# Attention's product with the values: turned so that the split exponentials are stationary and the split values move, with the seam before attention reordered

## The reference

```
def token_mixing(h, ...):
    z = h @ w_in
    qa, ka, va, cq, ckv, kr = split(z)
    qa, ka = rope(rmsnorm(qa)), rope(rmsnorm(ka))         # 8 query heads, 2 key heads, 64 wide
    oa = window_attention(qa, ka, va, swa_sink)           # keys of the tile before, the same and the next
    qb = (rmsnorm(cq) @ mla_w_uq)                         # 8 heads, 96 wide
    kv = (rmsnorm(ckv) @ mla_w_ukv)                       # k_nope and vb, 64 wide each
    kb = concat(k_nope, k_rope)
    qb, kb = rmsnorm and rope of both
    ob = dense_attention(qb, kb, vb)
    return concat(oa, ob) @ w_out

y = (silu(h @ wg) * (h @ wu)) @ wd                        # SwiGLU, before and behind; x += gate * y each time
```

## Time and profile before

| | |
|---|---|
| time, three runs | 3287.0 us median (3283.91 to 3290.35) |
| the profiled execution | 3284.61 us, span of the trace 3282.8 us |
| granted TensorE clock over the span | 0.983 of full speed |
| busy: PE / PEld / DVE / ACT / POOL | 96% / 75% / 44% / 25% / 16% |
| DMA | 207.51 MB, 63 GB/s mean |
| mixing by tiles | about 1280 to 1492 us |
| attention | about 1512 to 2033 us |
| output projection | from 2036 us |

### The profile page before, as it was taken

How to read it: one execution, slowest core, us unless ns; L and a number is a source line. 1 busy time by engine, 2 the same in 40 slices (tenths; PEclk the granted TensorE clock), 3 DMA queues, 4 the chain that set the end, 5 groups by cost and what they waited for, 6 DMA issues and landing times.

```text
span 3282.8 us, 39034 instructions
## 1 busy us (share of the span) xinstructions
PE 3156.4 (96%) x14017; PEld 2456.1 (75%) x14017; DVE 1458.5 (44%) x2512; ACT 809.3 (25%) x1422; POOL 522.0 (16%) x307
## 2 busy tenths in 40 slices
PE   7999999999999989996989998999999999999998
PEld 2688888888888868884545555878888888888887
DVE  2566666666662356874443332362322232322234
ACT  3311111011111145763433333331111111111112
POOL 1111111111111143320000001531111111111110
PEclk9999999999999999997989999999999999999999
DMA  7112122221221022445312122221011111011112
GB/s 245 39 57 69 40 77 66 62 64 55 60 67 37 27 79 63 139 138 138 91 39 60 50 69 74 84 71 33 26 38 32 32 32 32 26 38 32 32 32 84
DMA packets 268288, 207.51 MB, mean 63 GB/s; under 512 B 16956, under 2 KB 241071, under 8 KB 268207
## 3 DMA queue, kind: packets, MB, share of 16 engines
q1 hardware_dynamic: 268206, 206.41, 21.4%
HBM read 169.31 MB, written 37.06 MB: 63 GB/s over the span
## 4 chain that ended last, share of the span: by engine, by line
PE 53%; DVE 4%; issue 2%; ACT 1%; SPq 1%; DMA 1%; DVEq 0%; POOL 0%; ACTq 0%
PE PS L428 13%; PE PS L429 13%; PE PS L430 13%; PE PS L1454 6%; PE PS L1405 1%; PE PS L1439 1%; PE PS L1438 1%; PE PS L1440 1%; PE PS L1418 1%; DVE mbuf L1573 1%; PE PS L1394 1%; PE PS L1430 0%; SPq L1688 0%; PE PS L1431 0%; PE PS L1461 0%
## 5 line engine op out<-in xcount | busy, mean ns | idle before, releaser
L428 PE MATMUL PS<-H_hi,W_hi 128*128 128x512 f32 x2304 | 906.5, 393 | 8.0 <-POOL W_lo L1771 4.1
L430 PE MATMUL PS<-H_hi,W_lo 128*128 128x512 f32 x2304 | 898.5, 390 | 0.0
L429 PE MATMUL PS<-H_lo,W_hi 128*128 128x512 f32 x2304 | 897.9, 390 | 0.0
L422 POOL TENSOR_TENSOR W_lo<-raw,W_hi 128x1024 fp32r<-128x1024 f32 x132 | 316.1, 2402 | 1829.4 <-ACT W_hi L395 1829.4
L578 DVE SCALAR_TENSOR_TENSOR XT<-PS,mod,XT 128x512 f32<-128x512 f32 x528 | 395.4, 750 | 302.9 <-PE PS L430 302.7
L428 PEld LDWEIGHTS PS<-H_hi,W_hi 128*128 128x128 f32 x2304 | 433.7, 188 | 99.3 <-issue 11.1
L430 PEld LDWEIGHTS PS<-H_hi,W_lo 128*128 128x128 f32 x2304 | 433.3, 188 | 92.0
L429 PEld LDWEIGHTS PS<-H_lo,W_hi 128*128 128x128 f32 x2304 | 433.8, 188 | 90.0 <-issue 1.4
L564 DVE TENSOR_TENSOR PS<-hid_g,PS 128x512 f32<-128x512 f32 x132 | 91.8, 696 | 821.5 <-PE PS L430 810.4
L395 ACT ACTIVATE W_hi<-raw 128x1024 fp32r<-128x1024 f32 x132 | 137.2, 1055 | 1225.2 <-PE PS L430 1224.4
L428 PE MATMUL PS<-hid_hi,W_hi 128*128 128x512 f32 x1056 | 416.3, 394 | 6.5 <-DVE XT L578 5.1
(11 more groups left out here) (207 smaller groups left out, 3028.5 us busy)
## 6 DMA issues: line engine op xcount, KB each, us to landing
ada_r<-in_ada_w SPq DMA_DIRECT2D x192, 128.0 KB, 2.3
raw<-in_ffn_wg SPq DMA_DIRECT2D x44, 512.0 KB, 3.9
raw<-in_ffn_wu SPq DMA_DIRECT2D x44, 512.0 KB, 4.0
raw<-in_ffn_wd SPq DMA_DIRECT2D x44, 512.0 KB, 3.6
ada_w_sb<-in_ada_w SPq DMA_DIRECT2D x6, 2048.0 KB, 15.5
raw<-in_w_out SPq DMA_DIRECT2D x24, 512.0 KB, 4.2
scr_qb<-qT_st SPq DMA_DIRECT2D x24, 384.0 KB, 4.7
scr_kb<-kT_st SPq DMA_DIRECT2D x24, 384.0 KB, 6.2
```

What stands on the lines that cost most here:

```text
L422: pool.tensor_tensor(W_lo[:, n % WS, :], raw[:, n % RS, :], W_hi[:, n % WS, :].bitcast(F32), ALU.subtract).then_inc(w_ready, 1)
L428: pe.matmul(out, w_hi, m_hi, start=first, stop=False)
L429: pe.matmul(out, w_hi, m_lo, start=False, stop=False)
L430: return pe.matmul(out, w_lo, m_hi, start=False, stop=last)
```

## The change

The product with the values is turned round. The exponentials `e` are split into `p_hi` (ACT, a second pass) and `p_lo` (POOL, a subtraction), and the values into a high and a low part; for each 128 queries `p_hi` or `p_lo` is the stationary side and 66 or 64 columns of values move. The output lies with queries on partitions, so that the copy and the four transposes of the accumulator are gone. The product lags three steps where it lagged two. The low part of the dense values is made by DVE in the mixing stage and stored beside the high part (`VHL` = 130 columns a head instead of 66); the window values are split by POOL after their load. Room for the new buffers is found in `XT`: it is saved tile by tile to DRAM during mixing, and loaded back (two tiles at unit 8, the rest in the output projection). In SP's plan the window loads move behind `sp_m`, and the query loads behind `sp_t`; the transposes of the last tile's q and k move behind the first row maxima. ACT's copy of the values waits for the saving of the first two tiles, and `dve_turn` of unit 0 for the values' writes. The first unit's two pieces of maxima use different banks.

```diff
-QR, PR, MR = 4, 3, 5
+QR, MR = 4, 5
+ER, HR = 3, 4
+PV_LAG = 3
+VHL = 2 * VB + 2
...
 def act_m(act, u):
...
+            act.wait_ge(xt_kept, 32)
+            act.activation(vb_hl[:, :, 0:VB], kv[:, :, NOPE:NOPE + VB], ACT.Copy).then_inc(*aM.tick("v_copied"))
...
 def dve_m_norm(dve, u):
...
+            dve.wait_ge(aM.sem, aM.at(u, "v_copied"))
+            dve.tensor_tensor(vb_hl[:, :, VB + 2:VHL], kv[:, :, NOPE:NOPE + VB], vb_hl[:, :, 0:VB].bitcast(F32),
+                              ALU.subtract).then_inc(*vM.tick("v_lo"))
             dve.wait_ge(aM.sem, aM.at(u, "k_square"))
...
+        def sp_keep(sp, u):
...
+            sp.dma_start(scr_xt[bass.ds(u, 1)].rearrange("a p k c -> p (a k) c"), XT[:, :, tok(u)]).then_inc(xt_kept, 16)
...
-            turns(sp, [(sp_rope, 0), (sp_ropeb, 1), (sp_swa, 1), (sp_m, 2), (sp_t, 2), (sp_s, 1), (sp_z, 0)])
+            turns(sp, [(sp_rope, 0), (sp_ropeb, 1), (sp_m, 2), (sp_swa, 1), (sp_t, 2), (sp_swa_q, 1), (sp_s, 1), (sp_z, 0), (sp_keep, 0)])
...
 def pe_values(pe, un, t):
-            pe.wait_ge(exps_done, i + 1)
-            if t == 0 and un.u >= 1:
-                pe.wait_ge(acc_kept, un.u)
+            pe.wait_ge(p_lo_done, i + 1)
...
-            pe.matmul(PS[0:VW, 4, :], v, probs[:, i % PR, :], start=(t == 0), stop=(t == un.nk - 1)).then_inc(pv_done, 1)
-
-        def pe_back(pe, un):
...
+            if first and un.u >= 2:
+                pe.wait_ge(o_scaled, un.u - 1)
             for q in range(4):
-                mm = pe.transpose(PS[:, 5, q * VW:(q + 1) * VW], acc[0:VW, un.rd, q * P:(q + 1) * P], ident[0:VW, 0:VW])
+                out, by = PS[:, 4 + un.rd, q * VW:(q + 1) * VW], slice(q * P, (q + 1) * P)
+                pe.matmul(out, p_hi(i)[:, by], v_hi, start=first and q == 0, stop=False, skip_group_check=True)
+                pe.matmul(out[:, 0:VB], p_hi(i)[:, by], v_lo, start=False, stop=False, skip_group_check=True)
+                mm = pe.matmul(out, p_lo(i)[:, by], v_hi, start=False, stop=last and q == 3, skip_group_check=True)
+            mm.then_inc(pv_done, 1)
...
 def attention_pe(pe):
...
+            for i in range(N_ALL):
+                if i < len(steps):
+                    un, t = steps[i]
+                    pe_scores(pe, un, t)
+                if i < len(steps) and t == 0 and un.u + 1 < NU:
                     pe_max_turn(pe, units[un.u + 1])
+                if PV_LAG <= i < len(steps) + PV_LAG:
+                    pe_values(pe, *steps[i - PV_LAG])
+                for v in units:
+                    if i == done_at(v.u) + 2:
+                        pe_turn(pe, v)
+                for ahead, piece in maxes_at(i):
+                    pe_max(pe, ahead, piece)
...
 def act_exp(act, un, t):
+            if i >= ER:
+                act.wait_ge(p_lo_done, i - ER + 1)
+            act.activation(e_slot(i), PS[:, 2 + i % 2, :], ACT.Exp).then_inc(exps_done, 1)
+
+        def act_p_hi(act, i):
+            act.wait_ge(exps_done, i + 1)
+            if i >= HR:
+                act.wait_ge(pv_done, i - HR + 1)
+            act.activation(p_hi(i), e_slot(i), ACT.Copy).then_inc(p_hi_done, 1)
...
-        def act_acc(act, un):
...
 def attention_pool(pool):
...
+            swa_v_split(pool, 0, NT - 1)
+            for i, (un, t) in enumerate(steps):
...
+                pool.wait_ge(p_hi_done, i + 1)
+                if i >= HR:
+                    pool.wait_ge(pv_done, i - HR + 1)
+                pool.tensor_tensor(p_lo(i), e_slot(i), p_hi(i).bitcast(F32), ALU.subtract).then_inc(p_lo_done, 1)
...
 def swa_loads(sp):
...
+            sp.wait_ge(xt_kept, 16 * NT)
             swa_tiles(sp, 0, NT - 1, swa_landed)
-            for un in units[0:QR]:
-                load_q(sp, un)
...
 def attention_loads(sp):
...
+                    for t in range(2):
+                        sp.dma_start(XT[:, :, tok(t)], scr_xt[t]).then_inc(xt_front, 16)
...
 def wo_loads(sp):
...
+                if 1 <= i <= KD:
+                    if i == 1:
+                        sp.wait_ge(pv_done, len(steps))
+                    sp.dma_start(XT[:, i - 1, CH:TOK].rearrange("p (t c) -> p t c", c=P),
+                                 scr_xt[TPC:NT, :, i - 1, :].rearrange("t p c -> p t c")).then_inc(xt_back, 16)
```

More of the change, by code:

```diff
@@ L83, in build @@
         silu_c = sb(ctx, "silu_c", [P, KD, 2])
+        with ExitStack() as sX:
+            XT_r = sb(sX, "XT_r", [P, KD, TOK], F32R)
         XT = sb(ctx, "XT", [P, KD, TOK])
@@ L1271, in sp_swa, with sp_swa_q @@
                 swa_loads(sp)
+        def sp_swa_q(sp, u):
+            if isinstance(u, int) and u == NT - 1:
+                for un in units[0:QR]:
+                    load_q(sp, un)
         def turns(eng, plan, done=()):
@@ L1286, in turns @@
                 for stage, lag in plan:
-                    if 0 <= u - lag < NT:
+                    if 0 <= u - lag < NT and (stage, u - lag) not in done:
                         stage(eng, u - lag)
@@ L1360, in build, with done_at @@
         turn_no = {un.u: i for i, un in enumerate(turns_out)}
+        def done_at(u):
+            return last_step[u] + PV_LAG
+        N_ALL = len(steps) + 8
         def turns_until(u):
@@ L1380, in v_job, with max_bank, maxes_at @@
             return un.seq * (HB // 2) + un.head // 2
+        def max_bank(un, piece):
+            return 2 * piece if un.u == 0 else 0
+        def maxes_at(i):
+            if i >= len(steps) or steps[i][0].u + 2 >= NU:
+                return []
+            (un, t), ahead = steps[i], units[steps[i][0].u + 2]
+            return [(ahead, piece) for piece in range(ahead.pieces)
+                    if t == (piece + 4 if un.nk == 8 else min(piece, un.nk - 1))]
         def pe_max(pe, un, piece):
             a = maxes_before[un.u] + piece
-            if a >= 1:
-                pe.wait_ge(reds_done, a)
+            if a >= 2:
+                pe.wait_ge(reds_done, a - int(a == 2))
             pe.wait_ge(un.q_sem[un.slot], q_count(un.u))
             if un.swa and NT - 1 in un.keys:
-                pe.wait_ge(swa_last, 16 * 8)
+                pe.wait_ge(swa_last, 16 * 6)
             if un.swa:
@@ L1481, in attention_pe @@
             pe.wait_ge(ones_rows, 2)
[L1482 removed]
+            pe.wait_ge(swa_landed, 16 * 6)
             for un in units[0:2]:
@@ L1550, in attention_act @@
             act.wait_ge(sw_written, 16 * (NT + 1))
-            for un, t in steps:
-                act_exp(act, un, t)
-                if t == 0 and un.u + 1 < NU:
-                    act_max_row(act, units[un.u + 1])
-                if t == 1 and un.u >= 1:
-                    act_acc(act, units[un.u - 1])
-                if t == 1 and un.u >= 3:
-                    act_turn(act, units[un.u - 3])
-                if t == un.nk - 1 and un.u + 2 < NU:
-                    act_sink(act, units[un.u + 2])
-            act_acc(act, units[-1])
-            for un in units[-3:]:
-                act_turn(act, un)
+            for i in range(N_ALL):
+                if i < len(steps):
+                    un, t = steps[i]
+                    act_exp(act, un, t)
+                    if t == 0 and un.u + 1 < NU:
+                        act_max_row(act, units[un.u + 1])
+                    act_p_hi(act, i)
+                    if t == un.nk - 1 and un.u + 2 < NU:
+                        act_sink(act, units[un.u + 2])
+                for v in units:
+                    if i == done_at(v.u) + 3:
+                        act_turn(act, v)
         def dve_max(dve, un, piece):
```

160 lines of the change are left out of this document (83 added, 77 removed).

## The result

Measured in alternation, the changed kernel takes 3741.2 us (median of 4 runs, 3735.8 to 3748.0) and the kernel before 3287.3 (3283.9 to 3290.4): a ratio of 1.138, 95% interval 1.137 to 1.139. The forecast was 3367, with a range that ended at 3465. The profiled execution took 3744.7 us (span 3742.9).

The account below looks back on a forecast made before the run. The prediction took TensorE to bound the kernel, setting the time of attention's 224 steps. Its terms, 103 - 12 - 12 - 9 + 6 + 3 + 3 = +82 us on 3284.6, gave 3367 us, range 3320 to 3465.

Parts of the forecast that it names:

- The product: Attention, value product: 12 matmuls at 0.110 us, 1.32 us per step in place of 0.86; +103 us over 224 steps.
- the cheaper load: Rival, value product: new stationaries load in 0.062 us like the accumulator's transposes; about 3239 us, chance 0.10.
- the shared load: Rival, value product: the pair on one stationary shares a load, 1.0 us per step; 3295 us, within break-even's chance.
- no overlap: Rival, value product: load and stream do not overlap, 0.14 us per matmul; 3448 us, chance 0.04.
- break-even: Rival, value product: loads partly hidden, spacing near 0.08 us per matmul; 3286 us, no change, chance 0.05.
- The clock: TensorE in attention: forecast clock 1.00; rival has a third of steps at the lower level, about 3520 us, chance 0.07.
- Accumulator and unit changes: Attention: four transposes per unit go, -12 us; TensorE's waits for row maxima and o_sb shrink, -7 us.
- The 5 us that the clock was to give back: Around 1677 to 1703 us: half-speed stretches behind TensorE's waits shorten as the waits shrink; -5 us.
- ACT and POOL: Attention: second ACT pass and one POOL subtraction (1.30 us) per step lie beside TensorE's 2.02 us step; 0 us.
- The seam: Before attention: writes come first, query load is late next, from 1497; -9 us (-15 to +5), first exponential near 1515.
- The smaller additions: DVE subtraction in mixing +6 us, XT copies 0, loads at unit 8 +3, output projection and end of attention +3.
- The sum: Whole kernel: all terms together +82 us on the profiled 3284.6 us, giving 3367 us; forecast's chance 0.74.

Follow-up runs that it names:

- the run with twice the columns: Changed kernel with each value matmul streaming its moving tile a second time into unused columns of its bank; 3458.3 us, ratio to the kernel before 1.052.
- paired run: Changed kernel with TensorE's order alone altered: score passes of two steps together, then the value products of two steps; 3661.5 us.
- the XT-copies run: Kernel before plus only the writes of each XT tile to DRAM during mixing, read by nothing; 3287.4 us against 3289.0, ratio 0.9996.
- the mixed one: Changed kernel with TensorE's order alone altered: a step's value matmuls stand between its three score passes (3, then 6, then 3); 3743.1 us.
- the one with the long wait shortened: Changed kernel with the two loads of XT's front tiles issued after the last key and value load; 3730.0 us.
- the version as a whole: Changed kernel with values stationary again, split exponentials streaming 512 columns, XT front loads later, prompt-unit maxima one step earlier; 3256.5 us, ratio to the kernel before 0.990.
- the runs with more columns: Changed kernel with value tiles streamed twice (3458.3 us), first score pass issued three times (3551.9), or value tiles streamed twice and first score pass issued twice (3493.6).
- both additions: Changed kernel with each value matmul streaming its columns twice and the first score pass of a step issued twice; 3493.6 us.

## Why the prediction was wrong

**The product: right.** 12 matmuls at 0.11 us and a step near 2.0 (measured 2.06). A unit of 8 steps grew from 16.0 to 19.7 us on average (the latter in the run with twice the columns), 3.7 us; the forecast had 8 x 0.46 less 0.25 for the transposes, 3.4. That run shows that the 0.11 is the load's. This speaks against the cheaper load, the shared load, no overlap and break-even alike. The Trainium skill's 81 ns for a pair at 128 columns ("TensorE: Matmul & The Clock Gate", "Back-to-back issue gap") does not hold for this form: 0.11 us at 2.4 GHz, in the run with twice the columns at just those 128 columns, and 0.21 at 1.2.

**The clock: this step failed.** The forecast took 1.00 through attention. It had the mechanism among its rivals ("most of a step is loads with short streams, and no row has that"), but gave it 0.07, with a third of the steps and 3520 us as its far end. Measured are, after 1540 alone, 850 of the 963 us from first score to last product at 0.50, 380 us of loss. Even the far end of that rival fell 221 us short. Two readings led there. It argued from the waits, which would shrink, and took -5 us for it. The waits did shrink (next point), and TensorE was busy for 98% of the stretch at 0.50. And the step's time at the low level was put at twice 2.02 for a third of the steps, without a reason for a third. The steps of a stage are alike, so nothing in the rows bounded the case below the whole stage: all 224 steps at the low level would have given 224 x 2.02 = 452 us more, by the forecast's own price. The share of the load records is no sign either: in mixing they cover 105 of 120 us at 1.00, with 256 columns behind each load, and in the new stretch at 0.50 they cover 452 of 522, with 66. The prediction wrote down that no row had steps of this kind, and then gave that little weight. The Trainium skill ("TensorE: Matmul & The Clock Gate", "Part 1: The HAM clock gate") says that the clock follows how busy the engine has been. The paired run's 88 us, all busy and at 0.50, do not agree if busy is what the profile's row calls busy.

**Accumulator and unit changes: right in size, as far as it can be read.** The kernel before waited in attention 11.4 + 8.6 us in the earlier trace rows, and 6.5 more for maxima and sinks before L1418. The changed one waits 12.4 for maxima and sinks and 0.7 for o_sb, with 5.4 for H_lo where it was 1.5: some 10 less, against the 7 taken. At the low clock TensorE leaves the other engines more time, so part of this may be the clock's: in the run with twice the columns, mostly at 1.00, these waits come to 22.5, which is 5.5 less. The 5 us that the clock was to give back have the wrong sign.

**ACT and POOL: right.** The low part takes 1.27 us a step on POOL, and no product waited for it.

**The seam: too hopeful by 5.** The rows around it (as the earlier trace rows):

```profile
1502.41 0.60 ACT L1078 ACTIVATE XT_r<-PS 128x512 fp32r<-128x512 f32 x1 [0.17 <-PE PS L456]
...
1502.52 5.60 SPq L1296 DMA_DIRECT2D scr_qb<-qT_st  x2
...
1509.85 1.49 POOL L1722 CAST swa_v<-XT 128x704 fp32r<-128x704 f32 x2 [13.26 <-DMA XT<-scr_va]
1510.24 9.39 SPq L1761 DMA_DIRECT2D q_swa<-scr_sw  x12
...
1516.78 0.55 PE L1455 MATMUL PS<-swa_ka,q_swa 128*128 128x256 f32 x1 [14.40 <-DMA q_swa<-scr_sw]
...
1529.68 0.60 ACT L1580 ACTIVATE XT<-PS 128x512 f32<-128x512 f32 x1 [1.39 <-PE PS L1492]
```

ACT's wait of 11.56 is gone (0.17), as predicted, and the query load is late next, as predicted; but it is issued at 1510 and not at 1497: the window loads end at 1502 and the four writes of tile 10 take 7.7 us, not 5. TensorE waits 14.4 us for it. From the last transpose of the latents to the first exponential it is 48.4 us where it was 52.1: 4 gained, not 9. The first exponential is at 1529.7, not near 1515, because the mixing also ends later.

**The smaller additions.** Mixing: +4.0 of the +6 taken, none of it the copies; the rest of the part is DVE's subtraction and the wider value write, not separated. The mixing also began 5 us later in this execution, which no step explains; in the XT-copies run it began 2.7 us later with no loss of time in the end. The burst of loads at unit 8: 5.7 us against 3 (0 to 8). At the output projection the first matmul waits 4.1 us for W_lo in both kernels.

**The sum** without the clock: 3364 measured so, 3367 forecast; the run with twice the columns gives 3361, the paired one 3346, the mixed one 3354 and the one with the long wait shortened 3352, each profiled time less 0.45 of its time at 0.50. So one price explains all of them. That the sum of the parts comes within 3 us is in part luck. The first exponential came 5.3 us later (1529.7 against 1524.4), where the seam and mixing terms had it 3 earlier. From the first to the last exponential the kernel before takes 501 us; the changed one, with the loss at 0.50 taken off, some 566, so +65 (+73 in the run with twice the columns), where the terms for attention add up to +82. These misses go opposite ways.

## What to carry to other kernels

Before turning a product so that the long side becomes stationary, count columns streamed per load in the new step, and treat the TensorE clock as a term of the sum that can take the whole stage, not as a side case: it cost here 380 us, where all the rest of the change cost some 80. The three forms of the product that were run spent 850, 198 and 38 us at 0.50; other forms were not tried. The split itself was worth having with the sides left as they were: three passes of 512 columns in place of the float32 product took 1.3 us off a prompt unit of 16.0, and the version as a whole, with its reordered seam and loads, took 1% less time. When a stage sits at the low level, look at what the engine streams before looking at its waits.

## What was not expected of the hardware

The same step runs at either level, depending on what went before: with twice the columns, 150 us at 0.50, then 328 us at 1.00 on the same code. TensorE, with no idle time, fell to 1.2 GHz behind 24 short matmuls with loads and three score passes (the paired run, 1810.8 us), and rose behind eight passes of 512 columns and four transposes (1807.3). And an engine given more to do was faster by 283 us. What ends a low stretch of 133 to 184 us in the runs with more columns stays open. In the changed kernel (2214.6 us), with twice the columns (1872.4) and with both additions (1917.9), the rise stands less than 4 us behind the start of one group: four transposes of `o_sb`, two passes of row maxima and three or four score passes in a row. But in the changed kernel the same group stood at 1925 and 2104 us without a rise, so the group is not enough by itself.
